# One unit of the branch product, instead of two, behind the fourth turn of each retention head

## The reference, cut to what matters

```python
y_a, new_rwkv = _rwkv7_branch(za_mix, s_rwkv, p)
y_b, new_ret = _retention_branch(zb, s_ret, pos)
gates = jax.nn.sigmoid(zg.astype(jnp.float32)).reshape(bsz, t, 2, D_MODEL)
merged = (gates[:, :, 0] * (y_a.astype(h.dtype) @ p['w_branch_a'])
          + gates[:, :, 1] * (y_b.astype(h.dtype) @ p['w_branch_b']))
out = merged.astype(h.dtype) @ p['w_out']
```

## Time and profile before

| | |
|---|---|
| median of 3 runs | 4158.36 us (4155.36 to 4164.71) |
| the profiled execution | 4158.62 us, of it span 4156.8 us |
| mean granted TensorE clock | 0.983 |
| PE busy | 3955.0 us, 95% |
| DVE, ACT, POOL busy | 48%, 34%, 7% |
| retention heads of layer 0, layer 1 | about 1114 to 1456 us, 3197 to 3538 us |

### The profile page before, as it was taken

How to read it: one execution, slowest core, us unless ns; L and a number is a source line. 1 busy time by engine, 2 the same in 40 slices (tenths; PEclk the granted TensorE clock), 3 DMA queues, 4 the chain that set the end, 5 groups by cost and what they waited for, 6 DMA issues and landing times.

```text
span 4156.8 us, 84432 instructions
## 1 busy us (share of the span) xinstructions
PE 3955.0 (95%) x36004; PEld 3499.0 (84%) x36004; DVE 2014.5 (48%) x3239; ACT 1420.0 (34%) x2345; POOL 289.3 (7%) x463
## 2 busy tenths in 40 slices
PE   7999999999999998999989999999998999989998
PEld 6888888888876687999978888888888766979997
DVE  4544554554345545333355455555443455554344
ACT  4333344343322323222243333444333223232222
POOL 1000000000111021000000000000001110100000
PEclk9999999999999999999999999999999999999998
DMA  6222221222466473443332222222224665412222
GB/s 206 66 60 70 71 74 61 68 66 78 134 204 214 157 243 112 122 134 107 117 109 68 61 71 69 72 63 69 68 76 134 204 208 162 156 46 76 70 73 71
DMA packets 476464, 446.09 MB, mean 107 GB/s; under 512 B 18766, under 2 KB 408968, under 8 KB 475216
## 3 DMA queue, kind: packets, MB, share of 16 engines
q1 hardware_dynamic: 417136, 251.74, 20.0%
q0 software_dynamic: 41568, 155.70, 11.6%
q10 hardware_dynamic: 17408, 33.56, 2.2%
HBM read 344.48 MB, written 96.45 MB: 106 GB/s over the span
## 4 chain that ended last, share of the span: by engine, by line
PE 85%; DVE 8%; ACT 3%; issue 2%; DMA 2%; DVEq 0%; ACTq 0%; POOL 0%; SPq 0%
PE ps L803 82%; DVE scr L2062 4%; PE ps L807 3%; ACT scr L1496 2%; DVE h_lo L2062 1%; DVE w_lo L2075 1%; DMA scr<-in_ada_w_dram 1%; ACT w_hi L1509 1%; DVE lw L2062 1%; DVE scr L2064 0%; ACT L1496 0%; ACT scr L1649 0%; DMA scr<-in_x_sample_dram 0%; DVE acc L2062 0%; DMA w_raw<-in_w_ffn_down_dram 0%
## 5 line engine op out<-in xcount | busy, mean ns | idle before, releaser
L803 PE MATMUL ps<-h_hi,w_hi 128*128 128x320 f32 x4544 | 1105.0, 325 | 75.1 <-DVEq L2070 23.8
L803 PE MATMUL ps<-h_lo,w_hi 128*128 128x320 f32 x4544 | 1041.9, 311 | 0.0
L803 PE MATMUL ps<-h_hi,w_lo 128*128 128x320 f32 x4544 | 1041.4, 311 | 0.0
L803 PEld LDWEIGHTS ps<-h_hi,w_hi 128*128 128x128 f32 x4544 | 748.6, 190 | 163.4 <-issue 133.7
L803 PEld LDWEIGHTS ps<-h_lo,w_hi 128*128 128x128 f32 x4544 | 767.0, 190 | 0.0
L803 PEld LDWEIGHTS ps<-h_hi,w_lo 128*128 128x128 f32 x4544 | 766.1, 189 | 0.0
L803 PE MATMUL ps<-scr 64*64 64x64 f32 (+10 forms) x13248 | 679.3, 250 | 22.0 <-DVEq L2226 11.7
L803 PEld LDWEIGHTS ps<-scr 64*64 64x64 f32 (+4 forms) x13248 | 464.3, 141 | 218.1 <-issue 163.3
L1509 ACT ACTIVATE w_hi<-w_raw 128x1024 fp32r<-128x1024 f32 (+1 forms) x468 | 411.0, 878 | 685.0 <-PE ps L803 667.3
L2075 DVE TENSOR_TENSOR w_lo<-w_raw,w_hi 128x1024 fp32r<-128x1024 f32 (+1 forms) x468 | 469.5, 1003 | 252.5 <-ACT w_hi L1509 232.0
L1496 ACT ACTIVATE scr<-ps 128x256 f32<-128x256 f32 (+7 forms) x899 | 377.4, 420 | 573.1 <-PE ps L803 380.6
(11 more groups left out here) (155 smaller groups left out, 3010.8 us busy)
## 6 DMA issues: line engine op xcount, KB each, us to landing
w_raw<-in_w_in_dram SPq DMA_DIRECT2D x180, 512.0 KB, 3.8
scr<-in_ada_w_dram POOLq DMA_DIRECT2D x40, 1024.0 KB, 6.2
scratch_z<-scr SPq DMA_DIRECT2D x124, 320.0 KB, 2.2
scr<-in_state_ret_dram POOLq DMA_DIRECT2D x64, 512.0 KB, 4.9
out_dram<-scr ACTq DMA_DIRECT2D x64, 512.0 KB, 3.1
w_raw<-in_w_ffn_up_dram SPq DMA_DIRECT2D x64, 512.0 KB, 4.0
w_raw<-in_w_ffn_down_dram SPq DMA_DIRECT2D x128, 256.0 KB, 2.7
scr<-scratch_z POOLq DMA_DIRECT2D x24, 1280.0 KB, 9.0
```

The lines of the kernel that those rows point to most:

```text
L803: return pe.matmul(out, lhsT, rhs, start=start, stop=stop, skip_group_check=True)
```

## The change

One number of the table of points is changed: `in` takes one unit instead of two (head 0: two instead of four). As the units are dealt out in order, all that follow move by one place: in heads 1 to 3 tiles now end at `v4`, `v7`, `s1`, `s3`, `y1`, `y3`, `x2` and `end`, where they ended at `in`, `v6`, `s0`, `s2`, `y0`, `y2`, `x1` and `x3`. In head 0 the same places hold, with two units each. `end`, which took none, now takes the last unit (head 0: the last two) of tile 7, on PE, ACT and DVE alike.

```diff
-POINTS = {"in": 2, "v": 1, "s": 1, "y": 1, "x": 1, "t": 1, "z": 1, "lt": 0, "la": 2, "lb": 2, "lb6": 1, "uw": 1, "ca": 1, "cb": 1, "cb3": 3, "pre": 1, "pre1": 2, "pre2": 2, "post": 2, "end": 99}
+POINTS = {"in": 1, "v": 1, "s": 1, "y": 1, "x": 1, "t": 1, "z": 1, "lt": 0, "la": 2, "lb": 2, "lb6": 1, "uw": 1, "ca": 1, "cb": 1, "cb3": 3, "pre": 1, "pre1": 2, "pre2": 2, "post": 2, "end": 99}
```

## The result

The changed kernel takes 4189.26 us (median of four runs, 4185.43 to 4193.81) against 4160.55 (4155.36 to 4164.71): 28.7 us more, a ratio of 1.0067 with an interval of 1.0054 to 1.0080. The profiled execution has a span of 4183.6 us, 26.8 more than before's, and a mean granted clock of 0.978 against 0.983.

What follows compares the result with a forecast made beforehand. PE, busy 95% of the span, was taken as the bound, so only its waits could change. Two layers' waits (11.2 us) plus clock loss (8.4) gave 19.6, 4158.62 + 19.6 = 4178 us, range 4161 to 4190.

Steps and rivals of the forecast that it cites:

- The store: Between heads 0 and 1: `acc` saved late, `bb0`'s first copy waits for its landing, PE stands at `v6`; +5.2 us a layer.
- Rival B: The store still lands before the copy wants it, or the copy doesn't wait: 4163 us; chance 0.17.
- The turns: Fifth turn to first state step, heads 1 to 3: 7.32 us instead of 8.73, a gain of 1.41.
- Head 0's start: PE's idle becomes one stretch of about 9 us before the sixth turn; first state step comes 1.75 us earlier.
- `in` of heads 2 and 3: First unit waits for the read-out behind DVE's last rotation steps: 2.78 us late, a net 0.98 lost per boundary.
- Rival C: `in` keeps its old start, each boundary gains 1.80, no store wait or clock loss: 4143 us; chance 0.06.
- `y3` and `x1`: Read-out wait between them: +0.82 us in heads 0 and 3, no cost in heads 1 and 2, where PE waits anyway.
- +2.62: Head 3's added costs: +0.82 us for the read-out before `x1`, +1.80 for the unit done at the head's end.
- The clock: Slower PE clock after two long waits a layer, in heads 0 and 1: 2.5 us each, 8.4 in all.
- rival D: Shorter waits, three at `in` and two at `x1` a layer, may cost clock too: 4192 us; chance 0.15.
- A: The forecast itself: the store is on the path; 4178 us, by itself 4168 to 4188; chance 0.62.

Runs made afterwards that it cites:

- experiment 1: Changed kernel with head 0 taking four units at `in` again, as before the change: 4164.38 us against 4162.09, ratio 1.0010.
- experiment 2: Changed kernel with only head 0 new; heads 1 to 3 take two units at `in` as before: 4182.52 us against 4162.09, ratio 1.0054.
- experiment 3: Changed kernel with the store of `acc` saving one tile of eight, read back eight times: 4172.25 us against 4162.09, ratio 1.0027.
- experiment 5: Changed kernel, head 0 as before, DVE's read-out at `end` ahead of the last block's low part: 4143.99 us against 4161.7, ratio 0.9961.
- experiment 7: As experiment 5, with DVE's read-out at `y3` ahead of its rotation step there: 4144.17 us against 4161.7, ratio 0.9963.
- experiment 4: Changed kernel with DVE's `end` read-out ahead of the rotation's last two steps: 4166.77 us against 4162.09, ratio 1.0013.

## Why the prediction was right, and where its size was off

**The store** was the step that decided, and it held in every part: issued late, landing 9.7 us after its issue (9.1 taken), PE idle 5.83 and 5.90 (5.5 expected). Experiments 1 and 2 show that the loss goes with head 0, experiment 3 that it is the landing that is waited for. Rival B, the store still hidden, falls: the 2.4 us to spare were no match for an issue that moved by 9.9 us in layer 0 and 12.5 in layer 1, counted from head 0's first turns (some 10 forecast).

**The turns** gained what was said: the rows of 0.57 and 0.79 are gone from the turns of heads 1 to 3, and at full clock (experiment 5, head 2 of layer 1) it is 7.29 us from the fifth turn to the first state step, where 7.32 was forecast. **Head 0's start** has one wait of 9.39, where about 9 was forecast, and came out within 1.2 us in both layers.

**`in` of heads 2 and 3** waits for the read-out behind the rotation, as forecast, 2.04 and 2.12. At head 1 only 0.32 is left in both layers; two units stand at head 0's end and not one. Rival C, that nobody waits, falls for this kernel, and experiment 5 shows the condition that I gave for it: with the delay gone, the boundary is a gain. That 4144 was measured there and 4143 was C's number is chance, as head 0 is as before in that experiment.

**`y3` and `x1`**: the wait is there in heads 1 and 2 (1.93 to 1.95; 1.12 in layer 0's head 1, behind one of 1.04 for a state). As a wait it is off the path, which experiment 7 shows, but it wasn't free, as I had it: in head 2 of both layers the clock behind it cost 1.7 us. Head 3 came out 0.7 to 0.8 better than its +2.62.

**The clock** is the term that was too small. I charged it only behind the two long waits of a layer, and left the short ones to rival D, as half of ten. Behind the long waits the loss is near the 2.5 taken: 2.2 and 3.1 behind the store's (0.67 and 0.55 over 6.8 us), and in head 0 2.9 in layer 1 (0.75 over 11.7) but 1.3 in layer 0 (0.86 over 9.6). What I left out is the clock behind the four late starts, 10.1 us, and behind head 2's `y3`, 3.4. Not all of it is new time, as before had lost some clock itself on the way to head 2. Against the forecast's 19.6 the heads took 28.6, 9.0 more: 10.3 more on the way to heads 2 and 3, 1.2 more on the way to head 1, and 1.0 and 1.5 less at head 0's start and in head 3. Of the 10.3, 7.3 fall on the way to head 3, where PE's busy time shows that it is the clock.

So the case is A with a part of D, and the number shows it: 4189.3 lies above A's own 4168 to 4188, and inside the stated range, by less than 1 us, only because that took in the lower part of D. What misled me was the one row that I held against D, full pace behind 2.58 and 3.53 us in layer 1's head 0. In layer 0 of the same execution the same wait of 2.58 ended at 1127.33, and soon after it the clock was at 0.51 for 3.4 us:

```profile
1128.50:1131.90 3.40, 3.40 (x15) 3.40 (x14) 3.16 (x8) 0.00 (x0) 0.00 (x0) 0.51 0.24 86
```

The same instructions and the same wait can thus keep the clock or lose it, as behind `y3`. The late starts lost it each time: in the changed kernel and in experiments 1 and 3, twelve places of twelve, at 0.57 to 0.78 over some 6.7 us. With the wait gone (experiments 4 and 5) the clock is full in eight places of eight, so it is the wait that costs it there. Why these waits lose it every time, and others of their length only at times, is open. They stand behind a stretch in which PE had already paused 1.35 us and done only short transposes; that this makes the difference is not shown.

The Trainium skill's "DMA: Bandwidth & Descriptors", section Bandwidth, has its rates from loads into SBUF; the estimate from them was 6.2 to 7.7 us for this store, and 9.7 was measured. The Trainium skill's "TensorE: Matmul & The Clock Gate", section "A second HAM failure mode: psum-queue depth-cycling", tells of small pauses of PE between groups of matmuls that make the clock swing. The traces agree for the four late starts and two of the waits behind `y3`, more places than my forecast had, but not for every new wait.

## What to carry to other kernels

Moving a unit of work into an engine's wait moves its follow-up on every other engine as well: look for who waits for that follow-up, and what stands ahead of it in its engine's list, down to a store on a queue that nobody thinks of. Where one accumulator is shared, the read-out has to be put where its own engine idles; here 0.8 us of DVE's waiting took it for nothing. With that, and with head 0 left as it was, a change that had lost 28.7 us gained some 18. And a wait of 2 us on PE can cost more than 2 us: here the clock added 1.7 to 2.9 behind each.

## What was not expected of the hardware

A wait of 2.0 to 2.1 us was followed by some 6.7 us at a granted clock of 0.58 to 0.74 in four cases of four in the changed kernel, so it cost 1.7 to 2.9 us more behind it. Waits of 2.58 and 3.53 us elsewhere left full pace in layer 1 and not in layer 0, with the same instructions.

The store of 2560 KB took 9.7 us to land here and 9.1 before, and one of 320 KB at the same place 3.0: for an eighth of the bytes a third of the time.
